# The low half of a weight chunk as two GpSimd instructions instead of one

## The reference

```python
# first block
h = rms_norm(x, norm1_g)
u_a, v_a, val_b, gate_b = split(h @ w_in)                    # 4 x 512 columns
a_out = gelu(u_a) * (causal 128x128 mixing of layer_norm(gelu(v_a)) + b)   # gated branch, 4 heads
b_out = silu(group_norm(causal_conv31(val_b * sigmoid(gate_b))))          # convolution branch, 4 heads of 128
x = x + concat(a_out, b_out) @ w_out
x = x + square(relu(rms_norm(x) @ w_ff1)) @ w_ff2            # 1024 -> 4096 -> 1024
x = rms_norm(x, final_g)
# second block
proj = rms_norm(x) @ w_in_2       # queries, keys, values, an indexer; rope on most of them
o_a = attention over the 128 keys that the indexer scores highest   # 8 heads
o_d = differential attention, causal                                # 4 heads
x = x + rms_norm(concat(o_a, o_d) @ w_out_2)
x = x + rms_norm(square(relu(rms_norm(x) @ w_up_2)) @ w_down_2)
```

## Time and profile before

| what | value |
|---|---|
| median of 3 runs | 1210.16 us (1210.1 to 1210.83) |
| the profiled execution's own time | 1210.72 us |
| its span, first to last instruction | 1208.9 us |
| TensorE busy | 1175.2 us, 97% |
| VectorE busy | 621.7 us, 51% |
| ScalarE busy | 291.7 us, 24% |
| GpSimd busy | 711.4 us, 59% |
| mean granted TensorE clock | 0.989 |

### The profile page before, as it was taken

One profiled execution on the slowest core, in us unless ns is written; L12 is line 12 of the kernel. 1 busy time (PEld: TensorE's weight loads), 2 busy tenths in 40 slices (PEclk: granted clock), 3 DMA queues, 4 the chain that ended last, 5 costly groups with the idle time before them and its releaser, 6 DMA issues.

```text
span 1208.9 us, 15516 instructions
## 1 busy us (share of the span) xinstructions
PE 1175.2 (97%) x5346; PEld 934.5 (77%) x5346; DVE 621.7 (51%) x1004; ACT 291.7 (24%) x572; POOL 711.4 (59%) x431
## 2 busy tenths in 40 slices
PE   7999999999999999999997998999999999999997
PEld 5877678888888888877685776676788888888884
DVE  4999874540024544367799567746554001453113
ACT  5144162210002111110201355545331000211011
POOL 6879947666666666656454333224666666666651
PEclk9999999999999999999998999999999999999998
DMA  6321213232323233224332221112223232323201
GB/s 251 123 88 45 80 67 131 95 102 89 104 87 104 90 102 98 94 87 146 107 112 81 70 84 39 40 49 71 72 102 101 90 104 87 104 90 101 95 27 69
DMA packets 34319, 111.23 MB, mean 92 GB/s; under 512 B 4704, under 2 KB 4832, under 8 KB 34272
## 3 DMA queue, kind: packets, MB, share of 16 engines
q1 hardware_dynamic: 31056, 105.40, 26.3%
q10 hardware_dynamic: 3216, 5.21, 1.6%
HBM read 102.99 MB, written 2.10 MB: 87 GB/s over the span
## 4 chain that ended last, share of the span: by engine, by line
PE 84%; DVE 11%; issue 2%; ACTq 1%; ACT 1%; DMA 0%; POOL 0%; POOLq 0%; DVEq 0%; SPq 0%
PE bank L520 25%; PE bank L521 24%; PE bank L522 24%; DVE work L1784 2%; PE bank L869 2%; DVE max L1780 2%; DVE bank L1453 2%; ACTq L1186 1%; PE bank L631 1%; PE bank L883 1%; PE bank L911 1%; PE bank L907 1%; DVE ropey L1741 1%; PE bank L551 1%; PE bank L553 1%
## 5 line engine op out<-in xcount | busy, mean ns | idle before, releaser
L394 POOL TENSOR_TENSOR wl<-raw,wh 128x1024 fp32r<-128x1024 f32 x188 | 455.2, 2421 | 15.7
L391 POOL TENSOR_SCALAR wh<-raw 128x1024 fp32r<-128x1024 f32 x188 | 201.8, 1073 | 437.6 <-PE bank L522 315.3
L520 PE MATMUL bank<-xh,wh 128*128 128x512 f32 x840 | 338.7, 403 | 10.7 <-DVE xl L1404 7.8
L521 PE MATMUL bank<-xl,wh 128*128 128x512 f32 x840 | 328.9, 392 | 0.0
L522 PE MATMUL bank<-xh,wl 128*128 128x512 f32 x840 | 328.9, 392 | 0.0
L520 PE MATMUL bank<-uh,wh 128*128 128x512 f32 x576 | 225.9, 392 | 0.9 <-DVE ul L1503 0.9
L522 PE MATMUL bank<-uh,wl 128*128 128x512 f32 x576 | 224.2, 389 | 0.0
L521 PE MATMUL bank<-ul,wh 128*128 128x512 f32 x576 | 224.1, 389 | 0.0
L520 PEld LDWEIGHTS bank<-xh,wh 128*128 128x128 f32 x840 | 158.4, 189 | 66.3 <-issue 25.7
L522 PEld LDWEIGHTS bank<-xh,wl 128*128 128x128 f32 x840 | 158.7, 189 | 34.0
L521 PEld LDWEIGHTS bank<-xl,wh 128*128 128x128 f32 x840 | 158.8, 189 | 32.9 <-issue 2.2
(11 more groups left out here) (255 smaller groups left out, 1129.6 us busy)
## 6 DMA issues: line engine op xcount, KB each, us to landing
raw<-wstream SPq DMA_DIRECT2D x189, 512.0 KB, 3.3
x<-xT SPq DMA_DIRECT2D x8, 256.0 KB, 6.1
out<-x SPq DMA_DIRECT2D x8, 256.0 KB, 2.1
qi<-ropey ACTq DMA_DIRECT2D x16, 64.0 KB, 2.3
qd<-ropey ACTq DMA_DIRECT2D x16, 64.0 KB, 2.1
kd<-ropey ACTq DMA_DIRECT2D x16, 64.0 KB, 2.1
qa<-ropey SPq DMA_DIRECT2D x16, 64.0 KB, 2.0
ka<-ropey SPq DMA_DIRECT2D x16, 64.0 KB, 2.0
```

Source lines behind the costliest of these rows:

```text
L391: nc.gpsimd.tensor_scalar(wh[c][:], raw[c][:], 1.0, 1.0, ALU.mult, ALU.mult).then_inc(high_ready, 1)
L394: nc.gpsimd.tensor_tensor(wl[c][:], raw[c][:], wh[c][:].bitcast(F32), ALU.subtract).then_inc(split_ready, 1)
L520: mm(out, wh_, mh, start=start, stop=False)
L521: mm(out, wh_, ml, start=False, stop=False)
```

## The change

`low(c)` becomes `low(c, n)`: the subtraction is made in two instructions, columns 0 to 511 and 512 to 1023. A new semaphore left_split counts the left ones, and the right one waits for the left one of the same chunk. split_ready is counted up by the right one only. The wait for high_ready moves from the three callers into low. Chunk 0 is left as it was. Nothing else is changed.

```diff
+        left_split = sem("left_split")
...
-            def low(c):
-                nc.gpsimd.tensor_tensor(wl[c][:], raw[c][:], wh[c][:].bitcast(F32), ALU.subtract
+            def low(c, n):
+
+                left, right = slice(0, 512), slice(512, 1024)
+                pool.wait_ge(high_ready, n + 1)
+                nc.gpsimd.tensor_tensor(wl[c][:, left], raw[c][:, left], wh[c][:, left].bitcast(F32), ALU.subtract
+                                        ).then_inc(left_split, 1)
+                pool.wait_ge(left_split, n)
+                nc.gpsimd.tensor_tensor(wl[c][:, right], raw[c][:, right], wh[c][:, right].bitcast(F32), ALU.subtract
                                         ).then_inc(split_ready, 1)
...
             for c in range(1, SLOTS):
                 pool.wait_ge(raw_loaded[c], 16)
                 high(c)
-                pool.wait_ge(high_ready, c + 1)
-                low(c)
+                low(c, c)
...
                         high(c)
-                        pool.wait_ge(high_ready, i * SLOTS + (c + 1))
-                        low(c)
+                        low(c, i * SLOTS + c)
...
                 high(n % SLOTS)
-                pool.wait_ge(high_ready, n + 1)
-                low(n % SLOTS)
+                low(n % SLOTS, n)
```

## The result

The changed kernel took 1215.38 us (median of 12 runs, 1212.55 to 1217.9), the kernel before, run beside it, 1212.16 us (12 runs, 1210.1 to 1213.45). The ratio of the paired runs is 1.0034 [1.0024, 1.0043], 4.1 us slower (2.9 to 5.2); the two medians alone differ by 3.2 us. The forecast was 1212.3 us, 2.1 us slower, with a range up to 1214.3: the sign was right, the size was not, and the result lies outside the range. Of the 3.1 us between forecast and result, 2.0 us are no effect of the change: the three runs of the kernel before from which I started (1210.1 to 1210.83 us, median 1210.16) lay low against the 1212.16 us of all twelve, and the same kernel gave 1209.3 to 1214.4 us in later runs.

What follows compares the result with a forecast made beforehand. TensorE bounds the kernel, with GpSimd's full queue a second bound at 91 to 151 us. Terms 0.2 + 1.9 - 0.2 - 0.1 + 0.1, plus 0.2 for lock-outs, give +2.1 us on 1210.16: 1212.3 us, range 1210.1 to 1214.3.

Steps and rivals of the forecast that it cites:

- Where GpSimd's time counts: GpSimd's full queue, about 81 to 153 us, delays head_low(2)'s ul and TensorE's third head; elsewhere idle time mostly covers the cost.
- The term of the nine low halves: Full queue before head_low(2): 9 x 0.22 = 1.98 us less 0.1 slack, +1.9 us; bounds 0 and 2.7.
- lock-outs by VectorE: VectorE keeping GpSimd off the port, expected once on the queue's dearer side: +0.2 us.
- The slack of 0.1 us: At out1_heads' third head, ul ends 0.15 us before TensorE needs it; less than 0.1 us left after wake-up.
- The clock: Rival: half clock behind the new pause of some 1.6 us costs 1.7 us more, 1214.0 us; 20%.
- spares a slow-clock stretch elsewhere: Pauses that move later avoid a half-clock stretch elsewhere, making the kernel faster; 3% chance.
- The terms without the clock: Start, queue, VectorE pairs, factor matrix and lock-outs sum to +2.1 us.
- The pairs on VectorE: Rope operations L1741 and L1744 under low halves: the pair gains 0.2 us, not 1.1.
- the first scores: TensorE's 6.8 us wait at L869, behind VectorE's chain: -0.2 us; bounds -1.1 and +0.3.
- probs: Probs pair L1863 on VectorE, before L883: -0.1 us.
- the rival built on it: Both VectorE operations of a pair get through between halves, each pair gaining 1.12 us: 1210.1 us; 15%.
- The start and the factor matrix: Chunk 1's low half delays TensorE's start, +0.2 us (0 to 0.3); VectorE's factor matrix at 155.20 us, +0.1 (-0.1 to +0.25).

Runs made afterwards that it cites:

- e1: Changed kernel with chunks 15 to 23 keeping the whole low half, all others split: 1211.9 us, ratio 1.0003 to the kernel before.
- e2: Changed kernel with only chunks 15 to 23 split, the other 179 whole: 1214.4 us, ratio 1.0025 to the kernel before.
- e3: Changed kernel, all halves kept, with head_low(2) moved one chunk earlier in GpSimd's queue: 1211.07 us, ratio 0.9991 to the kernel before.
- e8: Kernel before, whole low halves, with only head_low(2) moved one chunk earlier in GpSimd's queue: 1211.37 us, ratio 1.0002.
- e5: Changed kernel without the right half's wait for the left half: 1213.32 us, ratio 1.0015 to the kernel before.
- r2: The kernel before, profiled again without any edit: 1211.17 us.
- r1: The changed kernel in another execution, no edit: 1217.05 us.
- e6: Changed kernel with each low half in four instructions of 256 columns, waits between them: 1217.46 us, ratio 1.0049 to the kernel before.
- e4: Changed kernel with three unread products put into TensorE's pause behind conv_center(3): 1213.98 us, ratio 1.0015 to the kernel before.
- r3: Another execution of the changed kernel with only chunks 15 to 23 split, no further edit: 1215.65 us.

## Why the prediction was wrong in size and right in mechanism

**Where GpSimd's time counts: right.** The full queue, its nine chunks, the ul at its end and the third head behind it came as forecast; e1, e2 and e3 show it from three sides. The work outside the queue (179 chunks) cost nothing measurable.

**The term of the nine low halves: undersized.** I took 9 x 0.22 less 0.1 of slack, and 0.2 for lock-outs by VectorE, 2.1 us. The queue grew by 2.58 us. An undisturbed pair costs 0.26 us (2.56 against 2.30 for the last one). The pair itself came as forecast: from the start of the left half to the start of the next instruction it is 2.62 us, the mean of the eight that VectorE leaves alone. What I had too long is the whole: I took its duration, 2.38 to 2.41 us, but the next instruction starts a little before its end, 2.36 us behind its start, the mean of seven. So 9 x 0.26 = 2.3 us; the remaining 0.3 us stand in the queue's other instructions, as lock-outs by VectorE (the one behind the factor matrix above took 1.69 us instead of 1.30). The slack of 0.1 us did not exist (e8). The Trainium skill, "GPSIMD Engine Reference" (Elementwise, side-by-side cycle accounting), by which I estimated 0.16 us of fixed cost, comes out right for the instruction alone (0.15 us, e5); the 0.11 us of the wait come on top.

**The clock: the step that failed.** The sum carries no term for it. I gave the fall behind the new pause 20%, because TensorE had kept its full clock at 2.59 of 3.4 us busy and three full products lay between the two pauses. I reasoned for a pause of 1.6 us. It was 2.96 us long: the third head came at 153.73 us and not near 153.1, and conv_center(3) was not late with it but 0.26 us early (149.75 against 150.01). TensorE was busy for 0.57 of 3.4 us, and the clock fell in four of five executions; behind the pause of e5, 1.40 us, which is near the one I had in mind, it did not fall. The price per fall was sized right, 1.57 us against my 1.7. The second fall at 533 (+1.47 us) was in none of my cases; whether it belongs to the change is open. The lost one at 831 (-1.01 us) I had only as "spares a slow-clock stretch elsewhere", and it is missing in r2 too. In size the rival was near: 1214.0 us is 3.8 us over the level that I started from, and 4.1 us were measured, though with the fall at 533 us in the traces, which it did not have.

**The terms without the clock: right in sum, in part by luck.** In the traces they add up to 0.30 - 0.56 + 3.12 - 0.12 - 0.15 - 0.21 - 0.34 = 2.0 us, against a forecast of 2.1. The start and the queue came 0.6 us dearer than I had them (2.86 against 2.3), and the factor matrix and the places behind 661 us made up for it (-0.82 against -0.2).

**The pairs on VectorE: right in kind, rough in size.** The two operations of the rope before:

```profile
L1741 DVE TENSOR_TENSOR ropey<-tmp,tmp 128x512 f32<-128x512 f32 x10 | 15.8, 1584 | 0.0
L1744 DVE TENSOR_TENSOR ropey<-tmp,tmb 128x512 f32<-128x512 f32 x10 | 8.9, 893 | 1.0
L1651 DVE TENSOR_TENSOR ul<-tmb,uh 128x512 f32 x64 | 121.8, 1903 | 90.2 <-ACT uh L1160 90.2
```

and after:

```profile
L1745 DVE TENSOR_TENSOR ropey<-tmp,tmp 128x512 f32<-128x512 f32 x10 | 9.1, 914 | 0.0
L1748 DVE TENSOR_TENSOR ropey<-tmp,tmb 128x512 f32<-128x512 f32 x10 | 12.3, 1233 | 1.0
L1655 DVE TENSOR_TENSOR ul<-tmb,uh 128x512 f32 x64 | 60.9, 951 | 90.2 <-ACT uh L1164 90.2
```

In the mean the first of a pair gains 0.67 us and the second loses 0.34; 0.33 us per pair is left. The means mix two sorts. Four of the ten pairs meet no GpSimd instruction and take 0.69 us twice, before and after. Of the other six, none has both operations short with the change: the second takes 1.59 or 1.60 us in each, because a half stands in its way (the right one in four, the left one in two), and the pair gains 0.55 us in the mean. The one that I worked out, at 579.51 us, gained nothing (3.17 us against 3.06). The delay at the first scores shrinks by 0.15 us (I had 0.2), at 785 us by 0.21 (not in the sum), at probs by 0.34 (I had 0.1). ul of the feed-forward stages takes half its time, 61 us of VectorE in all, and TensorE gets nothing of it: that is most of the 64.8 us by which VectorE's busy time fell. The exclusive port of the Trainium skill, "SBUF — State Buffer" (Who interferes with whom), fits these rows; the rival built on it, in which both operations get through, does not.

**The start and the factor matrix: small, as forecast.** +0.30 us, on its upper bound (I had 0.2), and -0.12, just past its lower one (I had +0.1, between -0.1 and +0.25).

**The base.** I took three runs within 0.06% of one another as the level, but the kernel's later runs spread over 0.4%. Part of this is the start: the full clock is first granted between 10.7 and 12.9 us in some executions and between 16.2 and 16.6 us in others (r1, e3 and e6). These come to TensorE's short wait near 116 us at 118.1 to 118.2, the others at 115.9 to 116.5 us. A range of 4.2 us was too narrow for an effect of 2 us on such a base.

## What to carry to other kernels

An instruction added to an engine at 60% load costs what it costs where that engine's queue is full: find the stretch without idle time, count the added instructions in it, and see who waits for its last job. If that job can go one place earlier, the price goes with it (e3). And a wait of 3 us on TensorE should be priced with the half clock behind it, as in four of five executions here, not at its length alone. The level itself needs more than three runs when the effect is as small as the spread.

## What the runs showed of the hardware that I had not expected

Filling the same slip with products that nobody reads (e4) was 2.3 us cheaper than leaving TensorE idle in it. The same program on different executions has its half-clock stretches in different places (e2 and r3 behind the pause, and at 530 us), so a fall seen in one profile is not yet a property of the kernel. And a wait of GpSimd on its own previous instruction cost 0.11 us.
